# Two transpose groups of each token tile issued as one, in a two-layer block kernel

## The reference

```python
for l in range(2):
    f = swiglu(rmsnorm(h, ffn1_pre_g[l]), ...)            # 1024 -> 2816 -> 1024
    h = h + 0.5 * rmsnorm(f, ffn1_post_g[l])
    u = rmsnorm(h, mix_pre_g[l])
    merged = ...  # stick-breaking, forgetting and memory attention of u, gated by sigmoid(u @ w_gate)
    h = h + rmsnorm(merged @ w_out[l], mix_post_g[l])
    f = swiglu(rmsnorm(h, ffn2_pre_g[l]), ...)
    h = h + 0.5 * rmsnorm(f, ffn2_post_g[l])
# second block
h = h + short_conv_mixer(rms_norm(h, a_mix_norm), ...)
h = h + conv_ffn(rms_norm(h, ffn_norm[0]), ...)
shared = shared_latent_kv(h, ...)
h = h + mla_attention(rms_norm(h, b_mix_norm), ..., shared)
h = h + conv_ffn(rms_norm(h, ffn_norm[1]), ...)
return rms_norm(h, final_norm)
```

## Time and profile before

| | |
|---|---|
| median of 3 runs | 1828.04 us (1827.88 to 1828.91) |
| the profiled execution's own time | 1827.37 us |
| its span, first to last instruction | 1825.3 us |
| granted clock of TensorE, mean | 0.999 |
| busy: TensorE matmuls | 1815.1 us, 99% of the span |
| busy: TensorE weight loads | 1623.0 us, 89% |
| busy: VectorE | 1421.4 us, 78% |
| busy: ScalarE | 1129.1 us, 62% |
| DMA queue of the weights | 331.57 MB, 60.5% of the 16 engines' span |

### The profile page before, as it was taken

One profiled execution on the slowest core, in us unless ns is written; L12 is line 12 of the kernel. 1 busy time (PEld: TensorE's weight loads), 2 busy tenths in 40 slices (PEclk: granted clock), 3 DMA queues, 4 the chain that ended last, 5 costly groups with the idle time before them and its releaser, 6 DMA issues.

```text
span 1825.3 us, 29155 instructions
## 1 busy us (share of the span) xinstructions
PE 1815.1 (99%) x10885; PEld 1623.0 (89%) x10885; DVE 1421.4 (78%) x2266; ACT 1129.1 (62%) x1953; POOL 225.0 (12%) x178
## 2 busy tenths in 40 slices
PE   9999999999999999999999999999999999999998
PEld 8888999998888888888999888888889998989997
DVE  7775747787797879787777788788768888768987
ACT  7664545555666666666555657665557765757764
POOL 0220001110032003200011102310002210002210
PEclk9999999999999999999999999999999999999999
DMA  8775575455576558655664548655746756536754
GB/s 245 218 221 179 173 193 172 142 153 179 166 230 193 175 172 231 194 175 163 194 179 147 185 140 232 194 165 182 224 145 196 206 165 192 175 116 187 209 164 146
DMA packets 436045, 333.91 MB, mean 183 GB/s; under 512 B 25402, under 2 KB 381504, under 8 KB 435904
## 3 DMA queue, kind: packets, MB, share of 16 engines
q1 hardware_dynamic: 435440, 331.57, 60.5%
q10 hardware_dynamic: 464, 0.47, 0.1%
HBM read 330.91 MB, written 1.05 MB: 182 GB/s over the span
## 4 chain that ended last, share of the span: by engine, by line
PE 97%; DVE 2%; ACT 1%; issue 0%; DMA 0%; ACTq 0%
PE bank L2024 16%; PE bank L2001 15%; PE bank L2003 15%; PE bank L2002 15%; PE bank L2012 7%; PE bank L2026 7%; PE bank L2014 7%; PE bank L2013 7%; PE bank L2030 2%; PE bank L2023 1%; DVE wlo L1289 1%; PE bank L2371 0%; PE bank L2437 0%; PE bank L2442 0%; PE bank L2408 0%; DVE U L1342 0%
## 5 line engine op out<-in xcount | busy, mean ns | idle before, releaser
L1289 DVE TENSOR_TENSOR wlo<-raw,whi 128x1024 fp32r<-128x1024 f32 (+3 forms) x634 | 744.4, 1185 | 177.2 <-ACT whi L700 170.5
L700 ACT ACTIVATE whi<-raw 128x1024 fp32r<-128x1024 f32 (+3 forms) x634 | 631.7, 1008 | 247.3 <-PE bank L2003 145.0
L2024 PE MATMUL bank<-U,whi 128*128 128x512 f32 x1280 | 439.1, 395 | 0.0
L2026 PE MATMUL bank<-U,wlo 128*128 128x256 f32 x1120 | 314.6, 281 | 0.0
L2012 PE MATMUL bank<-U,whi 128*128 128x256 f32 x1024 | 289.1, 282 | 0.0
L2014 PE MATMUL bank<-U,wlo 128*128 128x256 f32 x1024 | 286.2, 280 | 0.0
L2013 PE MATMUL bank<-U,whi 128*128 128x256 f32 x1024 | 285.6, 279 | 0.0
L2024 PEld LDWEIGHTS bank<-U,whi 128*128 128x128 f32 x1280 | 230.2, 188 | 42.3
L2001 PE MATMUL bank<-whi,U 128*128 128x384 f32 (+2 forms) x592 | 219.4, 371 | 0.1
L2026 PEld LDWEIGHTS bank<-U,wlo 128*128 128x128 f32 x1120 | 210.1, 188 | 6.9
L2002 PE MATMUL bank<-whi,U 128*128 128x384 f32 (+2 forms) x592 | 211.3, 357 | 0.0
(11 more groups left out here) (354 smaller groups left out, 2691.5 us busy)
## 6 DMA issues: line engine op xcount, KB each, us to landing
raw<-in_ffn_w_up SPq DMA_DIRECT2D x351, 256.0 KB, 3.5
raw<-in_ffn_w_down SPq DMA_DIRECT2D x264, 256.0 KB, 3.0
raw<-in_ffn_w_gate SPq DMA_DIRECT2D x175, 256.0 KB, 3.5
raw<-in_w_gate SPq DMA_DIRECT2D x128, 192.0 KB, 3.1
raw<-in_w_in SPq DMA_DIRECT2D x80, 256.0 KB, 3.8
raw<-in_a_w_in SPq DMA_DIRECT2D x48, 256.0 KB, 3.5
raw<-in_w_mem_kv SPq DMA_DIRECT2D x32, 256.0 KB, 3.4
raw<-in_w_out SPq DMA_DIRECT2D x32, 256.0 KB, 3.1
```

The costliest lines, as they stand in the source:

```text
L700: act.activation(whi[n % SLOTS][:, 0:w], unsplit(n, w), ACT.Copy).then_inc(hi_ready, 1)
L1289: dve.tensor_tensor(wlo[n % SLOTS][:, 0:w], unsplit(n, w), whi[n % SLOTS][:, 0:w].bitcast(F32), ALU.subtract).then_inc(lo_ready, 1)
L2024: ins = pe.matmul(dst, wh, u2[:, k, :], start=(k == 0), stop=(k == KT - 1))
L2026: pe.matmul(dst[:, 0:TOK], wl, uhi[:, k, :], start=False, stop=False)
```

## The change

The two transpose groups of a tile are issued one directly behind the other. In `tail` the first tile's two groups used to stand behind the third-last and the second-last chunk of the second tile; now both stand behind the second-last. In the next stage the second tile's two groups used to stand behind the third and the fourth chunk of the first tile; now both stand behind the third, at points 2, 3, 5, 6 (`glu_groups`), 4 (`mixer`) and 8. `both_turns` is a new helper. The loop of `conv_ffn` (points 7 and 9) and that of the memory projection (point 1) keep their two places for the second tile.

```diff
--- before.py
+++ after.py
@@ -2045,6 +2045,10 @@
                     ins = turn(src[:, t, nb * 512 + k * P:nb * 512 + (k + 1) * P], dst[:, k * P:(k + 1) * P])
                 ins.then_inc(ut_full, 1)
 
+            def both_turns(b, t):
+                for nb in range(2):
+                    stream_turn(b, t, nb)
+
             def u_ready(b, t, k):
                 pe.wait_ge(u_done, 16 * b + 8 * t + k + 1)
 
@@ -2082,8 +2086,9 @@
                         if j == n - 1 and nb == 0:
                             ins.then_inc(full, 1)
                     ins.then_inc(w_used, 1)
-                    if n - 3 <= j < n - 1:
-                        turns(j - n + 3)
+                    if j == n - 2:
+                        for nb in range(2):
+                            turns(nb)
 
             def last_tail(c, n, first, xh, xl, bank_ready):
 
@@ -2149,8 +2154,8 @@
                                 ins.then_inc(w_used, 1)
                             elif j == 3:
                                 ins.then_inc(gu0_full, 1)
-                            if t == 0 and j >= 2:
-                                stream_turn(b, 1, j - 2)
+                            if t == 0 and j == 2:
+                                both_turns(b, 1)
                 for g in range(1, groups):
                     if g >= 2:
                         pe.wait_ge(h_done, (count0 + g - 2) * TT + 2)
@@ -2329,8 +2334,8 @@
                             ins.then_inc(w_used, 1)
                         elif i == 3:
                             ins.then_inc(v0_full, 1)
-                        if l and t == 0 and i in (2, 3):
-                            stream_turn(b, 1, i - 2)
+                        if l and t == 0 and i == 2:
+                            both_turns(b, 1)
                 pe.wait_ge(rb_done, 2 * b + 2)
                 for t in range(TT):
                     ins = turn(rb[:, t, :], bank[4][:, ts[t]])
@@ -2601,8 +2606,8 @@
                         ins.then_inc(w_used, 1)
                     elif j == 3:
                         ins.then_inc(lat0_full, 1)
-                    if t == 0 and j >= 2:
-                        stream_turn(8, 1, j - 2)
+                    if t == 0 and j == 2:
+                        both_turns(8, 1)
             def latent_keys(j):
                 start_chunk(c_kv + j)
                 for t in range(TT):
```

## The result

The changed kernel takes 1840.36 us (median of 4 runs, 1838.56 to 1841.17) against 1827.96 for the kernel before (1827.46 to 1828.91, 4 runs). The ratio is 1.0067, 95% interval 1.0054 to 1.0080: 12.4 us slower. The forecast was 1838.1 in a range of 1833.0 to 1841.5.

The account below looks back on a forecast made before the run. TensorE was taken to bound the kernel, busy 1815.1 of 1825.3 us. Losses at points 2 to 9 summed to 10.2, less 0.1 for joins; 1827.37 became 1837.5, plus 0.67 for the median: 1838.1 us, range 1833.0 to 1841.5.

Parts of the forecast that it names:

- The mechanism: At point 2: first tile's group 1.38 us later delays ScalarE, VectorE and the second tile's additions; TensorE waits, losing 1.17.
- The two edits make the loss together: At point 2: the later first-tile group takes the cover away, the earlier second-tile group spends it; 1.17 us lost.
- Points 2 to 7 and 9: Losses claimed: 1.17 us at points 2 and 5, 1.26 at 3, 1.94 at 4, 1.39 at 6, 1.28 each at 7 and 9.
- Point 8: No post-norm there; late copies delay both tiles' operands, the second's by some 0.5 us; loss 0.7, between 0.2 and 1.0.
- A join by itself: Joined eight transposes cost 0.88 us, as do two fours; rounding leaves 0.00 to 0.04 saved per join, 15 joins.
- the sum: Losses at points 1 to 9 total 10.2 us, less 0.1 for joins: 10.1 us.
- 36 transposes (nine groups of four, one at each of points 1 to 9) come six matmuls later: First tile's first-half groups at points 1 to 9 move later, taken as 1.38 us; no work added or removed.
- take the delay up: Rival, 0.07: ScalarE and VectorE absorb the delay at point 2; only point 4 waits, 0.6 us; time 1828.6.
- half of it: Rival, 0.05: a delay of 0.7 us in place of 1.38 gives some 5 us; time 1833.
- Four transposes behind four others: Rival, 0.03: transposes right behind others cost nothing, so 15 joins save 6.6 us; time 1821.4.
- The clock rival: Rival, 0.05: TensorE's new waits drop the clock to 1.2 GHz at seven points, 9.8 us more; time 1848.
- The argument against it: Against a clock fall: TensorE already idles 0.88 us at 1594.36 with granted clock 1.00, the 2.4 GHz level.

Follow-up runs that it names:

- the halves: Two kernels, each the kernel before with one edit: first tile's groups joined later, 1835.15 us; second tile's groups joined earlier, 1828.33 us; kernel before 1827.64.
- filling that hole: Changed kernel with the next stage's fourth-chunk split ahead of the turned stream's first half on ScalarE and VectorE: 1831.50 us against 1827.64 for the kernel before.
- the two other kernels that have both waits: Changed kernel with the first tile's groups apart again, ahead of points 7 and 9 (1836.93 us) or at the two merges (1837.91 us).

## Why the prediction was right

**The mechanism held, step by step.** The first tile's late group passes whole through ScalarE and VectorE into the second tile's additions: at point 2 ScalarE's idle time grew by 1.39 us and VectorE's by 1.28, and filling that hole took back 7.4 of the 11.4 us, by place. The second tile's last addition is 1.38 late against TensorE (485.98 less 0.92, against 483.68), as forecast, and misses TensorE, which now wants the second half 1.4 us earlier. "The two edits make the loss together" is shown by the halves: 0.28 and -0.01 at point 2 alone, 1.17 together.

**The terms.** Points 2 to 7 and 9 were forecast at 9.49 us and measured 9.33, none off by more than 0.08. Point 8, called an estimate between 0.2 and 1.0 and taken at 0.7, measured 0.53: about 0.1 at the first tile's first matmul, where 0.2 was expected, and 0.4 at the second tile's, where it was 0.5. A join by itself was priced at 0.00 to 0.04 us saved; point 1, the one place with a join and no wait, gained 0.05, and eight transposes take 1.03 from the first start to the last end, 0.43 more than four.

**What the sum missed.** The step "36 transposes (nine groups of four, one at each of points 1 to 9) come six matmuls later" counts too few. `tail` serves the two merges as well, so it is eleven groups and seventeen joins, and the merges cost 1.54 us by the same mechanism. The code of `mixer` shows the call; I had read the callers that turn the stream and not those that turn `M`. By place the changed kernel lost 11.36 us where the sum had 10.1, so the merges are all of these 1.3 us and cover some 0.3 by which the other terms were too high. The other 1.0 of the 2.3 us between 1838.1 and 1840.36 is at no place: the profiled execution took 1838.56, and the median of its four lies 1.8 above that, where 0.67 was added for it. Its cause is open. The range was wide enough for both, but no case in it was this one; that the time still fell inside is luck in this part.

**The rivals.** ScalarE and VectorE did not take the delay up, nor half of it: 1.38 us arrived, and the two edits cost 3.5 us more together than apart. Four transposes behind four others are not free, 0.43 us against the 0.44 of a group apart, so nothing gets faster. The clock rival was given 0.05 as a fall at all seven points. It happened at one place, in one of the four traces with both waits of point 4. The argument against it, an idle time of 0.88 us at full clock, held for the single waits of these traces: the 1.4 us ahead of the group at points 7 and 9 left the clock at 1.00 in all five traces that have them. Point 4 has two with 0.66 us of transposes between, a case that the rows of before did not have. The Trainium skill, page "TensorE: Matmul & The Clock Gate", section "Why this matters for your kernels", ties a loss of clock to idle gaps longer than any of these, by which point 4 would have lost nothing to it; the measurement decides, and here the clock fell once behind two short ones and cost 1.5 us.

## What to carry to other kernels

Before moving an instruction in a queue, follow what its signal starts on the other engines, in their order, down to the next thing that comes back: a signal that came 1.4 us later was 1.4 us later everywhere behind, as long as no engine on the way had a hole. Two edits that are each nearly free can use the same cover, one by making an operand late and the other by wanting it early; price them together. When a helper is changed, list all its callers, and where a moved signal opens a hole on another engine, put independent work into it.

## What the runs showed that I had not expected

The granted clock fell to 0.50 for 3.4 us behind two idle times of 1.01 and 0.73 us with four transposes between, in one of the two traces of the changed kernel, whose waits agree to 0.01 us, and in neither of the two other kernels that have both waits; what decides it is open. A single idle time of 1.4 us was not followed by it in any trace. And the loss at a place repeats to 0.02 or 0.03 us between executions and between different kernels, where whole executions differ by 1 to 2 us: the comparison of two traces place by place settled here what the medians of five runs could not.
